# Strassen's scheme for 19 of 22 pairs of column blocks in the up projection of a hybrid decoder layer

## Chip, cores and metric

One core of one Trainium2 chip. The metric is the device time of one execution in microseconds.

## What is computed

One decoder layer on x of 1024 tokens by 1024 channels, float32: a mixer (gated DeltaNet, sparse attention and a convolution, with one input and one output projection), then the gated MLP, with which this case deals:

```python
def conv_gated_mlp(x, w_up, conv_w, w_down):      # x (1024, 1024), w_up (1024, 5632), conv_w (3, 5632), w_down (2816, 1024)
    h = causal_dwconv(x @ w_up, conv_w)           # 3 taps along the tokens, a channel at a time
    gt, val = jnp.split(h, 2, axis=-1)
    return (jax.nn.silu(gt) * val) @ w_down

h = rms_norm(x, norm_ffn_pre)
x = x + rms_norm(conv_gated_mlp(h, ffn_w_up, ffn_conv_w, ffn_w_down), norm_ffn_post)
```

## The kernel before, in words

The kernel is written by hand, with a queue for each engine and a semaphore wait before each instruction that needs one; `LATE` gives late stages semaphores that early ones have done with. In time order: input projection and convolutions, the mixer (a fixed interleaving of steps), output projection with both norms, up projection (from about 700 us), down projection (from about 1024 us).

**Operands in two parts.** A float32 matmul is made of two: each operand is split in a rounded high part and a low part. For a weight block, ACT writes the high part (`up_split_hi`, L1759: a copy with scale 1 - 1/64) and POOL the low part (`up_split_lo`, L1763: block minus high part). For the normed tokens h2, ACT writes h2_p (scale 1/64, L1657) and DVE h2_q (L1686). The matmul of high parts and that of low parts add up in PSUM to 1/64 of the product; the convolution's taps carry the factor 64.

**Up projection.** Channels lie on partitions, tokens along the free dimension. There are 22 pairs j of column blocks of 128: unit u = 2j is the gate block, u = 2j + 1 the value block. `up_products` (L1697) does a unit: 8 blocks k of the contraction, high and low, 2 halves of 512 tokens, so 32 matmuls of 128 x 512. A pair has four PSUM banks, and pairs take turns with the two sets of four. The first halves of units 0 to 2 are done in the stage before, between the last turns of tokens (`up_begin`); `up_pe` does the rest. After a unit ACT applies the last tap from PSUM into an SBUF tile (L1783), then splits the unit u + 3 (L1759), and after a value unit does the silu (L1795); DVE adds the other two taps, reading PSUM and the SBUF tile (L1814, L1817); POOL makes the low part of unit u + 3 (L1763) and after a value unit the product of gate and value (L1807), which stays in SBUF in `act_f[j]` for the down projection. SP loads unit u as soon as the staging tile is free (L1747), 512 KB. PE waits for the low part of its unit, and for the taps of the unit four back, whose banks it takes.

**Down projection.** Two halves of 512 tokens, m = 0 and 1, each with 22 blocks k: `kk` = 22 m + k. A step kk has 16 matmuls (L1980): four tiles of 128 tokens, high and low, two halves of 512 columns. ACT splits the high parts of the row block of w_down (L1849, 1024 columns) and of the activation (L1869, 512 columns), DVE the low parts (L1854 and L1873; POOL does L1854 for kk = 0 to 2). SP loads the rows of w_down (L1878) four steps ahead, and at kk = 8 and 37 the residual x1 (four tiles of 512 KB).

```python
            for k in ks:
                for w, x in ((up_p[up_slot(u)], h2_p), (up_q[up_slot(u)], h2_q)):
                    for h in halves:
                        ins = pe.matmul(up_ps[j % 2][:, g, h * 512:(h + 1) * 512], w[:, k], x[:, k, h * 512:(h + 1) * 512],
```

## Time and profile before

| | us |
|---|---|
| median of three runs | 1199.31 (1198.91 to 1199.84) |
| the profiled execution, its own time | 1199.23 |
| its span in the profile | 1197.2 |
| PE busy | 1148.0 (96%) |
| DVE busy | 707.1 (59%) |
| ACT busy | 566.3 (47%) |
| POOL busy | 367.0 (31%) |
| mean granted TensorE clock | 0.992 of full |

The time of an execution is 2.0 us longer than the span, which runs from the first to the last recorded instruction. Busy time is the time in which at least one instruction of an engine is under way; matmuls overlap one another, so a matmul's own duration (0.39 us for 512 columns) is longer than the distance from one to the next. A duration of an instruction runs from its issue to the engine to its end, with any wait inside the engine in it; waits on semaphores are not in it.

### The profile page before, as it was taken

To read this page: it belongs to the slowest core of one execution; us is meant where nothing else is said; L and a number is where in the kernel's file an instruction comes from. 1 tells how busy PE (TensorE), PEld (TensorE's weight loads), DVE (VectorE), ACT (ScalarE), POOL (GpSimd) and SP (SyncE) were. 2 spreads that over 40 slices of the span, in tenths; PEclk is the share of its full clock that TensorE was granted. 3 is DMA by queue.
4 is the path that set the end of the run, shared out by engine and by line. 5 is a ranking of instruction groups with operands and counts; after the bars stand their busy time and mean duration, and the time that the engine had idled before them with its cause. 6 is when DMAs were issued, how large, how long until landed. Compare 5 with 4: busy or idle time off the path is not lost.

```text
span 1197.2 us, 22879 instructions
## 1 busy us (share of the span) xinstructions
PE 1148.0 (96%) x9530; PEld 950.1 (79%) x9530; DVE 707.1 (59%) x982; ACT 566.3 (47%) x1053; POOL 367.0 (31%) x378
## 2 busy tenths in 40 slices
PE   5999999899999999999998999999999999999996
PEld 5878879788877877878767878888888888888885
DVE  5798976546668785767546744333333333655744
ACT  7544333447565556465565644333333334545443
POOL 2476346122122131120232025444555554200000
PEclk9999999999999999999998999999999999999999
DMA  8345121410000000000114452222222221654651
GB/s 252 84 113 182 59 52 27 103 31 22 3 22 22 2 22 22 2 2 2 38 52 160 146 171 82 77 71 71 71 71 71 73 80 58 235 169 123 228 193 71
DMA packets 104079, 99.86 MB, mean 83 GB/s; under 512 B 15413, under 2 KB 89385, under 8 KB 103977
## 3 DMA queue, kind: packets, MB, share of 16 engines
q1 hardware_dynamic: 102536, 93.15, 25.6%
q10 hardware_dynamic: 1440, 5.24, 1.1%
q8 instruction: 77, 1.26, 0.4%
q14 instruction: 26, 0.21, 0.1%
HBM read 85.24 MB, written 13.11 MB: 82 GB/s over the span
## 4 chain that ended last, share of the span: by engine, by line
PE 84%; DVE 10%; ACT 3%; DMA 1%; issue 1%; POOL 0%; ACTq 0%; DVEq 0%
PE psum L1697 26%; PE psum L1980 14%; PE psum L1344 8%; PE psum L2516 6%; PE psum L1591 5%; PE psum L1524 4%; PE psum L2556 4%; PE psum L1540 4%; DVE arena L2403 3%; PE psum L1505 2%; PE psum L1337 1%; PE psum L1271 1%; PE psum L1289 1%; PE psum L1504 1%; PE psum L1425 1%
## 5 line engine op out<-in xcount | busy, mean ns | idle before, releaser
L1697 PE MATMUL psum<-h_p,up_p 128*128 128x512 f32 x704 | 221.0, 390 | 1.3 <-DVE arena L1673 0.7
L1697 PE MATMUL psum<-h_q,up_q 128*128 128x512 f32 x704 | 220.7, 389 | 0.0
L1814 DVE SCALAR_TENSOR_TENSOR arena<-psum,arena 128x1023 f32<-128x1023 f32 x44 | 56.4, 1283 | 196.1 <-ACT arena L1783 196.1
L1763 POOL TENSOR_TENSOR up_q<-arena,up_p 128x1024 fp32r<-128x1024 f32 x44 | 105.9, 2407 | 212.8 <-ACT up_p L1759 212.8
L1697 PEld LDWEIGHTS psum<-h_p,up_p 128*128 128x128 f32 x704 | 132.2, 188 | 29.4 <-POOL up_q L1763 1.1
L1697 PEld LDWEIGHTS psum<-h_q,up_q 128*128 128x128 f32 x704 | 132.2, 188 | 27.3
L1783 ACT ACTIVATE arena<-psum,arena 128x1024 f32<-128x1024 f32 x44 | 49.1, 1117 | 198.9 <-PE psum L1697 198.9
L1344 PE MATMUL psum<-arena 64*64 64x64 f32 x3072 | 110.8, 221 | 2.6 <-DVE arena L1120 1.5
L1980 PE MATMUL psum<-dn_p,ap_p 128*128 128x512 f32 x352 | 110.2, 394 | 3.2 <-DVE ap_q L1873 3.2
L1344 PEld LDWEIGHTS psum<-arena 64*64 64x64 f32 x3072 | 97.5, 134 | 17.8 <-issue 6.8
L1980 PE MATMUL psum<-dn_q,ap_q 128*128 128x512 f32 x352 | 109.9, 394 | 0.0
L2516 PE MATMUL psum<-h_p,cm_p 128*128 128x512 f32 (+1 forms) x288 | 87.3, 374 | 4.1 <-ACT arena L2280 2.3
L1026 ACT ACTIVATE arena<-psum 128x384 f32<-128x384 f32 x132 | 60.4, 489 | 59.9 <-PE psum L1524 59.2
L2516 PE MATMUL psum<-h_q,cm_q 128*128 128x512 f32 (+1 forms) x288 | 86.7, 372 | 0.0
L1228 DVE TENSOR_REDUCE arena<-psum 128x1 f32<-128x640 f32 (+7 forms) x96 | 66.9, 705 | 32.0 <-PE psum L1509 30.2
L1854 DVE TENSOR_TENSOR dn_q<-arena,dn_p 128x1024 fp32r<-128x1024 f32 x41 | 51.4, 1254 | 57.0 <-ACT dn_p L1849 57.0
L1019 ACT ACTIVATE arena<-psum,arena 128x640 f32<-128x640 f32 (+7 forms) x96 | 67.1, 701 | 34.7 <-DVE arena L1228 34.0
L1980 PEld LDWEIGHTS psum<-dn_p,ap_p 128*128 128x128 f32 x352 | 66.6, 189 | 18.1 <-DVE dn_q L1854 3.6
L1849 ACT ACTIVATE dn_p<-arena 128x1024 fp32r<-128x1024 f32 x44 | 46.6, 1058 | 71.5 <-PE psum L1980 66.5
L1980 PEld LDWEIGHTS psum<-dn_q,ap_q 128*128 128x128 f32 x352 | 66.7, 189 | 14.8
L2403 DVE SCALAR_TENSOR_TENSOR arena<-psum,arena 128x1023 f32<-128x1023 f32 (+29 forms) x60 | 75.9, 1264 | 1.4
L2516 PEld LDWEIGHTS psum<-h_p,cm_p 128*128 128x128 f32 x288 | 54.9, 191 | 14.8 <-issue 2.5
(299 smaller groups left out, 2172.4 us busy)
## 6 DMA issues: line engine op xcount, KB each, us to landing
arena<-in_ffn_w_up SPq DMA_DIRECT2D x44, 512.0 KB, 3.8
arena<-in_ffn_w_down SPq DMA_DIRECT2D x44, 512.0 KB, 3.7
arena<-in_w_in SPq DMA_DIRECT2D x20, 512.0 KB, 3.8
arena<-in_x SPq DMA_DIRECT2D x16, 512.0 KB, 5.6
qkv_mid<-arena ACTq DMA_DIRECT2D x9, 512.0 KB
arena<-qkv_mid SPq DMA_DIRECT2D x8, 576.0 KB, 4.2
arena<-in_w_out SPq DMA_DIRECT2D x8, 512.0 KB, 3.8
x_mid<-arena SPq DMA_DIRECT2D x8, 512.0 KB, 3.3
```

Of the source, the lines that this page charges most:

```text
L1019: act.activation(probs(u), s_psum(u, n), ACT.Exp, bias=nmx[:, u % 2:u % 2 + 1], accum_out=psums[:, NH * kind + h:NH * kind + h + 1]).then_ ...
L1026: act.activation(pt[x % 2].rearrange("p g c -> p (g c)"), psum[:, bank, 0:GDIM], ACT.Copy).then_inc(done, 1)
L1228: v.tensor_reduce(nmx[:, u % 2:u % 2 + 1], s_psum(u, n), AX.X, ALU.max, negate=True).then_inc(sem("n_mx"), 1)
L1344: ins = pe.matmul(out[rows, h * CH:(h + 1) * CH], lhs[rows, h], rhs[rows, h], start=start, stop=True, skip_group_check=True)
L1591: ins = pe.matmul(wm_ps[WM_SLOT[t]][:, n * 512:(n + 1) * 512], x[:, k], w[:, n * 512:(n + 1) * 512], start=first and k == ks[0] and w is w ...
L1697: ins = pe.matmul(up_ps[j % 2][:, g, h * 512:(h + 1) * 512], w[:, k], x[:, k, h * 512:(h + 1) * 512], start=k == 0 and x is h2_p, stop=Tru ...
L1763: pool.tensor_tensor(up_q[up_slot(u)], up_st[up_slot(u)], up_p[up_slot(u)], ALU.subtract).then_inc(late("up_lo")[0], 1)
L1814: v.scalar_tensor_tensor(out=y[:, 1:S], in0=ps[:, 0:S - 1], scalar=tap(1, u), in1=y[:, 1:S], op0=ALU.mult, op1=ALU.add).then_inc(late("up_ ...
L1854: eng.tensor_tensor(dn_q[kk % 4], dn_st[kk % 4], dn_p[kk % 4], ALU.subtract).then_inc(late("dn_lo")[0] if kk < 3 else sem("dn_lv"), 1)
L1980: ins = pe.matmul(dn_ps[t % HT][:, n * 512:(n + 1) * 512], x[:, tok], w[:, n * 512:(n + 1) * 512], start=first and x is ap_p[s], stop=True ...
L2403: own.up(v.scalar_tensor_tensor(out=cacc[:, c, s:S], in0=glu[c][:, 0:S - s], scalar=w, in1=cacc[:, c, s:S], op0=ALU.mult, op1=ALU.add))
L2516: ins = pe.matmul(cm_ps[i % 2][:, c0:c1], w[:, k], x[:, k, c0:c1], start=k == 0 and x is h_p, stop=True, skip_group_check=True)
```

## The change

Pairs 0 to 2 stay as they are (`CLASSIC = 3`). For the pairs j = 3 to 21 the product [gate | value] = W^T h is taken as one of 2 x 2 blocks: gate and value block, lower and upper half of the contraction (kh), first and second half of the tokens (th). Seven products of half size (4 blocks k, high and low, 512 tokens: 8 matmuls) take the place of eight, in the variant with running sums: U = P1 + P6, U + P7 and U + P7 + P4 are formed in one PSUM bank, each copied out by ACT before the next product adds to it; P2 and P5 + P3 have banks of their own, which DVE adds.

- Once, during the classic pairs: h2 is laid out by halves of tokens; DVE rebuilds four quarters of it (`whole`, 128 x 2048 each) and forms differences (two on DVE, two on POOL), and the four combined operands T5, T6, T7 and T4 are split by ACT (`t_hi`) and DVE (`t_lo`).
- For each pair: SP loads both blocks (`pair_load`, 2 x 512 KB). DVE makes four sums of weight quarters (`weight_sum`, 128 x 512, all operands in SBUF). ACT and POOL split seven slabs of 128 x 512 (`split_mult_hi`, `split_mult_lo`), in a ring of five. ACT copies four results of 128 x 512 out of PSUM (`copied`), DVE adds three more from PSUM onto these (`added`). The convolution then reads the copy in SBUF (`c_a`, `c_b`) and no longer PSUM: ACT the last tap (`tap_a`, `tap_b`), DVE the other two, for gate and value. ACT does the silu, POOL the product.
- The product goes into one of two tiles, and SP stores it in DRAM (`spill`, 512 KB), but for pairs 0 to 2 and 21. In the down projection SP loads it back by halves of tokens (`act_reload`, 256 KB, 36 times), one with each step's load of w_down. The first three reloads wait until the last product of the up projection is done.

```diff
+CLASSIC = 3
+MULTS = [(1, CLASSIC)]
+for _j in range(CLASSIC, NF):
+    MULTS += [(i, _j) for i in (5, 6, 2, 7)] + [(1, _j + 1)] * (_j + 1 < NF) + [(i, _j) for i in (4, 3)]
+PRODUCTS = len(MULTS)
+RING = 5
...
+        mult_ps = lambda i, j: psum[:, 4 * (j % 2) + {1: 0, 6: 0, 7: 0, 4: 0, 2: 1, 5: 2, 3: 2}[i], :]
...
+        def split_mult_hi(act, i, j):
+            n = mult_at(i, j)
+            if n >= RING:
+                act.wait_ge(*late("up_mm", 2 * CLASSIC + n - RING + 1))
...
+            act.activation(slab_p[n % RING], sum_source(i, j), ACT.Copy, scale=1.0 - SPLIT_W).then_inc(late("up_hi")[0], 1)
...
+        def split_mult_lo(pool, i, j):
+            n = mult_at(i, j)
+            pool.wait_ge(*late("up_hi", 2 * CLASSIC + n + 1))
+            pool.tensor_tensor(slab_q[n % RING], sum_source(i, j), slab_p[n % RING], ALU.subtract).then_inc(late("up_lo")[0], 1)
...
+            t_hi(5, 0, "t_f", 3)
+            classic_tap(0)
+            up_split_hi(act, 3)
+            classic_tap(1)
+            up_split_hi(act, 4)
+            silu(0)
+            t_hi(7, 1, "t_pool", 1)
...
+            for j in range(CLASSIC, NF):
+                more = j + 1 < NF
+                if j > CLASSIC:
+                    tap_b(j - 1)
+                if more:
+                    split_mult_hi(act, 1, j + 1)
+                if j > CLASSIC:
+                    tap_a(j - 1)
+                else:
+                    silu(CLASSIC - 1)
+                split_mult_hi(act, 4, j)
+                copied(6, j)
+                split_mult_hi(act, 3, j)
+                if more:
+                    split_mult_hi(act, 5, j + 1)
...
+                copied(7, j)
+                if j > CLASSIC:
+                    silu(j - 1)
+                if more:
+                    split_mult_hi(act, 6, j + 1)
+                    copied(1, j + 1)
+                    split_mult_hi(act, 2, j + 1)
+                copied(4, j)
+                if more:
+                    split_mult_hi(act, 7, j + 1)
...
+            for j in range(CLASSIC, NF):
+                more = j + 1 < NF
+                if more:
+                    split_mult_lo(pool, 1, j + 1)
+                if j == CLASSIC:
+                    prod(CLASSIC - 1)
+                split_mult_lo(pool, 4, j)
+                split_mult_lo(pool, 3, j)
+                if more:
+                    split_mult_lo(pool, 5, j + 1)
...
+                if j > CLASSIC:
+                    prod(j - 1)
+                if more:
+                    for i in (6, 2, 7):
+                        split_mult_lo(pool, i, j + 1)
...
+            def conv(c, y, u, count):
+                v.wait_ge(*late("up_tap", count))
+                v.scalar_tensor_tensor(out=y[:, 1:S], in0=c[:, 0:S - 1], scalar=tap(1, u), in1=y[:, 1:S],
+                                       op0=ALU.mult, op1=ALU.add).then_inc(late("up_c1")[0], 1)
+                v.wait_ge(*late("up_c1", count))
+                v.scalar_tensor_tensor(out=y[:, 2:S], in0=c[:, 0:S - 2], scalar=tap(0, u), in1=y[:, 2:S],
+                                       op0=ALU.mult, op1=ALU.add).then_inc(late("up_conv")[0], 1)
+
+            def conv_b(j):
+                conv(c_b[j % 2], y_b[j % 2], 2 * j + 1, 2 * j + CONV_B)
...
+            def added(i, j):
+
+                mult_done(v, i, j)
+                src, dst = {2: (1, c_a[j % 2][:, left]), 5: (7, c_b[j % 2][:, right]), 3: (6, c_a[j % 2][:, right])}[i]
+                copy_done(v, src, j)
+                v.tensor_tensor(dst, dst, mult_ps(i, j), ALU.add).then_inc(late("c_add")[0], 1)
...
+            for j in range(CLASSIC, NF):
+                more = j + 1 < NF
+                if j > CLASSIC:
+                    added(3, j - 1)
+                if more:
+                    weight_sum(5, j + 1)
+                if j > CLASSIC:
+                    conv_b(j - 1)
+                    conv_a(j - 1)
+                added(2, j)
+                if more:
+                    weight_sum(6, j + 1)
...
+                added(5, j)
+                if more:
+                    weight_sum(7, j + 1)
+                    weight_sum(3, j + 1)
...
+            for n, (i, j) in enumerate(MULTS):
+                pe.wait_ge(*late("up_lo", 2 * CLASSIC + n + 1))
...
+                elif i in (6, 7):
+                    copy_done(pe, {6: 1, 7: 6}[i], j)
+                elif i == 4:
+                    copy_done(pe, 7, j)
+                    pe.wait_ge(*late("t_lo", 4))
+                elif i == 3:
+                    add_done(pe, 5, j)
+                for k in range(HT):
+                    for w, x in ((slab_p[n % RING], x_p[i]), (slab_q[n % RING], x_q[i])):
+                        ins = pe.matmul(mult_ps(i, j), w[:, k], x[:, k], start=k == 0 and x is x_p[i] and i not in (6, 7, 3, 4),
+                                        stop=True, skip_group_check=True)
+                ins.then_inc(late("up_mm")[0], 1)
...
+            for kk in range(4, DN):
+                dn_ready(sp, kk - 4)
                 down_load(sp, kk)
+                if kk + 2 in RELOADS:
+                    act_reload(sp, kk + 2)
```

## Rows read from the trace of the kernel before

**Rows 1.** The page's first part: busy us (share of the span) and instructions of each engine.
```profile
PE 1148.0 (96%) x9530; PEld 950.1 (79%) x9530; DVE 707.1 (59%) x982; ACT 566.3 (47%) x1053; POOL 367.0 (31%) x378
```

**Rows 2.** The chain of waits in order of time: start, us, engine, what, line.
```profile
714.10 1.23 DVE h_q L1686
715.38 308.60 PE psum L1697 x1360
1023.98 146.47 PE psum L1980 x640
1170.53 1.06 ACT dn_p L1849
1173.59 16.56 PE psum L1980 x64
```

**Rows 3.** Stretches of the up projection: busy us (instructions), clock, DMA share, GB/s.
```profile
core 0: us, PE busy (x) PEld busy (x) DVE busy (x) ACT busy (x) POOL busy (x), PEclk, DMA share, GB/s
...
900.00:950.00 50.00, 50.00 (x222) 41.40 (x222) 17.95 (x14) 17.30 (x17) 24.30 (x11) 1.00 0.24 70
```

**Rows 4.** Instructions in order of time, 866 to 869 us, DVE and POOL.
```profile
866.59 2.40 POOL L1763 TENSOR_TENSOR up_q<-arena,up_p 128x1024 fp32r<-128x1024 f32 x1 [4.84 <-ACT up_p L1759]
866.91 1.28 DVE L1817 SCALAR_TENSOR_TENSOR arena<-psum,arena 128x1022 f32<-128x1022 f32 x1
```

**Rows 5.** Instructions in order of time, 1026 to 1033 us, DVE and POOL.
```profile
1026.16 2.41 POOL L1854 TENSOR_TENSOR dn_q<-arena,dn_p 128x1024 fp32r<-128x1024 f32 x1 [4.85 <-ACT dn_p L1849]
...
1027.69 1.43 DVE L1873 SCALAR_TENSOR_TENSOR ap_q<-ap_p,arena 128x512 fp32r<-128x512 f32 x1
1028.51 2.88 POOL L1807 TENSOR_TENSOR arena<-arena 128x1024 f32<-128x1024 f32 x1
...
1029.96 2.51 DVE L1854 TENSOR_TENSOR dn_q<-arena,dn_p 128x1024 fp32r<-128x1024 f32 x1 [0.84 <-ACT dn_p L1849]
```

**Rows 6.** Durations by line: some with min/median/max ns, others busy us and mean ns.
```profile
L1697 PEld LDWEIGHTS psum<-h_p,up_p x704: 186/188/190, 699.6 to 1022.9; 128*128 128x128 f32 x176
...
L1854 DVE TENSOR_TENSOR dn_q<-arena,dn_p x41: 1210/1225/2511, 1030.0 to 1171.6; 128x1024 fp32r<-128x1024 f32 x41
...
L1873 DVE SCALAR_TENSOR_TENSOR ap_q<-ap_p,arena x44: 677/684/1431, 1020.4 to 1172.8; 128x512 fp32r<-128x512 f32 x44
...
L1160 DVE TENSOR_TENSOR arena<-arena x8: 546/548/1927, 327.4 to 631.4; 128x384 f32<-128x384 f32 x8
...
L1681 DVE SCALAR_TENSOR_TENSOR arena<-arena x8: 1275/1278/1285, 655.3 to 709.7; 128x1024 f32<-128x1024 f32 x8
...
L1807 POOL TENSOR_TENSOR arena<-arena x22: 2392/2412/2882, 727.5 to 1028.5; 128x1024 f32<-128x1024 f32 x22
...
L2076 POOL TENSOR_TENSOR vc_q<-arena,vc_p x2: 1287/1290/1293, 211.8 to 213.1; 128x512 fp32r<-128x512 f32 x2
...
L1133 DVE TENSOR_TENSOR arena<-psum,arena 128x384 f32<-128x384 f32 x40 | 22.2, 556 | 6.9 <-PE psum L1344 3.6
...
L1783 ACT ACTIVATE arena<-psum,arena 128x1024 f32<-128x1024 f32 x44 | 49.1, 1117 | 198.9 <-PE psum L1697 198.9
...
L1869 ACT ACTIVATE ap_p<-arena 128x512 fp32r<-128x512 f32 x44 | 27.0, 616 | 0.0
...
L1795 ACT ACTIVATE arena<-arena 128x1024 f32<-128x1024 f32 x22 | 23.1, 1052 | 0.0
...
L2122 ACT ACTIVATE kT<-psum 128x512 fp32r<-128x512 f32 x8 | 4.7, 592 | 0.2 <-PE psum L2142 0.2
```

**Rows 7.** Instructions in order of time, 630 to 634 us, POOL and DVE.
```profile
630.55 2.35 POOL L898 TENSOR_TENSOR wo_q<-arena,wo_p 128x1024 fp32r<-128x1024 f32 x1 [0.54 <-ACT wo_p L1051]
...
631.38 1.93 DVE L1160 TENSOR_TENSOR arena<-arena 128x384 f32<-128x384 f32 x1 [0.60 <-ACT arena L992]
```

**Rows 8.** A stretch of the down projection, columns as in rows 3.
```profile
1040.00:1060.00 20.00, 20.00 (x89) 16.39 (x88) 10.68 (x12) 8.12 (x11) 0.00 (x0) 1.00 0.74 276
```

**Rows 9.** The page's part on DMA issues: count, KB each, median us to landing.
```profile
x_mid<-arena SPq DMA_DIRECT2D x8, 512.0 KB, 3.3
```

**Rows 10.** PE after idling (instructions in order of time), and a stretch, columns as in rows 3.
```profile
1173.59 0.70 PE L1980 MATMUL psum<-dn_p,ap_p 128*128 128x512 f32 x2 [3.16 <-DVE ap_q L1873]
1174.13 0.99 PE L1980 MATMUL psum<-dn_q,ap_q 128*128 128x512 f32 x2
1174.92 1.05 PE L1980 MATMUL psum<-dn_p,ap_p 128*128 128x512 f32 x2
1175.78 1.05 PE L1980 MATMUL psum<-dn_q,ap_q 128*128 128x512 f32 x2
...
632.00:636.00 4.00, 2.64 (x8) 2.25 (x9) 3.18 (x4) 1.81 (x2) 0.89 (x1) 0.50 0.44 132
```

More of the change, by code:

```diff
@@ L284 @@
     "f_rs": ("tap0", 17),
-    "dn_hi": ("w_hi", 80),
+    "dn_hi": ("w_hi", 36 + 2 * CLASSIC + PRODUCTS),
     "ap_hi": ("rope_tab", 2),
@@ L317, with build @@
     "x1r3": ("gp_in", 32),
+    "sw_st0": ("x_in2", 64),
+    "sw_st1": ("x_in3", 64),
+    "t_f": ("k_lo", 8),
+    "t_pool": ("q_lo", 8),
+    "t_hi": ("k_hi", 8),
+    "t_lo": ("q_hi", 8),
+    "s_add": ("g_ss", 8),
+    "c_cp": ("g_rs", 8),
+    "c_add": ("c_ss", 8),
+    "act_st0": ("wck_in", 32),
+    "act_st1": ("wcv_in", 32),
 }
-def build(nc, a, out, scratch, qkv_mid):
+def build(nc, a, out, scratch, qkv_mid, act_mid):
     ctx = ExitStack()
@@ L1777, in up_act, with classic_tap @@
                 act.wait_ge(sem(f"x1_st{s}"), 16 * NT // 2)
-            for u in range(NU):
+            def classic_tap(u):
                 j, g = divmod(u, 2)
@@ new lines, in copied @@
+            def copied(i, j):
+                mult_done(act, i, j)
+                dst = {1: c_a[j % 2][:, left], 6: c_a[j % 2][:, right], 7: c_b[j % 2][:, right], 4: c_b[j % 2][:, left]}[i]
+                if i == 1 and j >= CLASSIC + 2:
+                    conv_done(act, j - 2, CONV_A)
+                if i == 1 and j == CLASSIC:
+                    act.wait_ge(*late("up_prod", 2))
+                if i == 7 and j >= CLASSIC + 2:
+                    conv_done(act, j - 2, CONV_B)
+                if i == 7 and j == CLASSIC:
+                    act.wait_ge(*late("up_prod", 3))
+                act.activation(dst, mult_ps(i, j), ACT.Copy).then_inc(late("c_cp")[0], 1)
@@ new lines, in tap_b, with tap_a @@
+            def tap_b(j):
+                add_done(act, 5, j)
+                copy_done(act, 4, j)
+                if j >= CLASSIC + 2:
+                    spilled(act, j - 2)
+                act.activation(y_b[j % 2], c_b[j % 2], ACT.Copy, scale=tap(2, 2 * j + 1)).then_inc(late("up_tap")[0], 1)
+            def tap_a(j):
+                add_done(act, 3, j)
+                add_done(act, 2, j)
+                if j >= CLASSIC + 2:
+                    act.wait_ge(*late("up_prod", j - 1))
+                act.activation(y_a[j % 2], c_a[j % 2], ACT.Copy, scale=tap(2, 2 * j)).then_inc(late("up_tap")[0], 1)
@@ new lines, in up_act @@
+            t_hi(5, 0, "t_f", 3)
[5 more added lines that the diff above has]
+            t_hi(7, 1, "t_pool", 1)
+            classic_tap(2)
+            up_split_hi(act, 5)
+            t_hi(6, 2, "t_f", 6)
+            classic_tap(3)
+            silu(1)
+            split_mult_hi(act, *MULTS[0])
+            classic_tap(4)
+            split_mult_hi(act, *MULTS[1])
+            split_mult_hi(act, *MULTS[2])
@@ L1823, in up_pe @@
         def up_pe(pe):
             pe.wait_ge(*late("v_lo", NT))
-            for u in range(NU):
+            for u in range(2 * CLASSIC):
                 pe.wait_ge(*late("up_lo", u + 1))
```

314 lines of the change are left out of this document (256 added, 58 removed).

## The prediction

> **What bounds the kernel now.** I read the page's busy shares first: PE is busy for 96% of the span [rows 1]. An average over stages proves little, so the chain of waits comes next. From 715.38 us it is one unbroken piece of up-projection matmuls of 308.60 us (1360 of them, 0.227 us each), followed directly by the down projection from 1023.98 us [rows 2]. So in the stage to be changed TensorE alone sets the pace, and an edit that removes matmuls shortens it, if no other engine then becomes slower than PE. The table of stretches says how much room the others have: in 50 us of the steady up projection DVE is busy 18.0, ACT 17.3 and POOL 24.3 us, with the clock at its full 2.4 GHz level [rows 3].
>
> One detail decides more than those shares. In the steady stage a POOL split (866.59 to 868.99) and a DVE tap (866.91 to 868.19) lie on top of each other and each takes its usual time, 2.40 and 1.28 us [rows 4]; that tap reads one operand from PSUM and one from SBUF. At the end of the stage, where DVE operates on two SBUF operands, it is otherwise. POOL works from 1026.16 to 1028.57; a DVE instruction issued at 1027.69 takes 1.43 us, not its median of 0.68, and ends 0.55 after POOL's end. The next POOL multiply, issued at 1028.51, takes 2.88 instead of 2.41 and ends 2.27 after DVE's end; the DVE subtraction behind it takes 2.51 instead of 1.23 and ends 1.08 after POOL's [rows 5, 6]. Far away, at 631.38, it is the same: 1.93 us instead of 0.55, ending 0.41 after POOL [rows 6, 7]. So a DVE instruction with two SBUF operands and a POOL tensor_tensor exclude each other; the one that waited runs 0.13 to 0.14 us shorter than alone once it is let in. Of the pairs of this sort that I read, none overlapped freely.
>
> **What the change does, part by part.**
> PE: a pair of column blocks has 2 x 8 x 2 x 2 = 64 matmuls of 512 columns; seven products of 4 x 2 make 56. At 0.227 us a pair goes from 14.5 to 12.7 us, and 19 x 8 = 152 matmuls fewer are 34.5 us less, the whole gain. Each product has weights of its own, where two matmuls in a row shared them, but a weight load stands beside every matmul already (as many as matmuls, 0.19 us each, under a pitch of 0.227 [rows 3, 6]): nothing.
>
> ACT per pair: seven slab splits of 512 columns at 0.62, four copies out of PSUM at 0.59, two taps at 1.12, one silu at 1.05 [rows 6]: 10.0 us, under 12.7.
>
> DVE per pair: three additions of a PSUM bank to one SBUF operand (0.56 for 384 columns, so some 0.69 for 512), four sums of weight blocks with both operands in SBUF (between 0.55 for 384 and 1.23 for 1024: 0.68), and the four convolution taps of 1.28 [rows 6]. 2.1 + 2.7 + 5.1 = 9.9 us, also under 12.7. But the taps now read c_a or c_b, which lie in SBUF, where they read PSUM. Eight DVE instructions a pair now have two SBUF operands, 7.8 us; there was none.
>
> POOL per pair: seven slab subtractions of 512 columns at 1.29 and one product of 2.41 [rows 6]: 11.5 us, under 12.7 by itself.
>
> The sum that matters is of the two that exclude each other: 11.5 + 7.8 = 19.3 us a pair, above both 12.7 and the old 14.5. From this go 0.135 us for each of the 16 instructions that had to wait; if they take turns throughout, 17.15. Do they? DVE's queue is in order: sum, addition, four taps, addition and so on, and with POOL always having a slab to do, each two-operand DVE instruction waits for one POOL instruction, eight against eight. DVE's three additions and the waits of the others fall beside POOL's work. Behind a held tap stand DVE's later additions, and PE's last product of a pair waits for one of them (P5), so PE idles some 5 us a pair. Bounds: 17.15 (turns throughout, nothing idle) and 20.3 (no gain at hand-over, 1 us in which neither works). I take 17.9, two of three hand-overs with the gain, being nearer to the rows, in which every waiting instruction had it.
> The Trainium skill, "SBUF — State Buffer", Who interferes with whom, says that a VectorE instruction with two SBUF inputs and a GpSimd instruction that reads SBUF hold a shared port as an exclusive lock, and the second to issue fully blocks until the first is done. The trace agrees that it is exclusive; read literally the rule would give 19.3 us a pair, since it knows no shortening, where the rows give 17.15 with turns throughout. The measured 0.13 us decides.
>
> Start of the stage: the classic units need 3 x 3.6 + 3 x 7.3 = 32.7 us of PE, as before. Beside them come, on DVE, four halves of 2048 columns rebuilt, two differences, four low parts (each 2048 columns, two SBUF operands, about 2.3 us: 0.68 + 3 x 0.53), four weight sums; on POOL two differences of 2048 (2.41 + 2 x 1.12 = 4.6 each), three splits and three products of 2.41 and five slabs. Exclusive work: 25.7 + 30.3 = 56 us, a bound from below; DVE's queue with all POOL work before it is 41 + 30 = 71, from above. Walking the queues in order with these durations, unit 3 waits for its low part until 729, unit 4 until 743, unit 5 until 751 (POOL's 4.6 us difference and DVE's sums alternate), the first slab is ready at 765, and the last product of the first pair ends 68 us after 715.4. ACT, too, holds unit 0's tap behind a high part that waits for three DVE instructions.
> Then 18 x 17.9 = 322: the up projection ends at 715.4 + 68 + 322 = 1105.6, against 1024.0: +81.6 us.
>
> End of the stage: DVE's last addition, four taps and their waits for POOL's two splits of w_down end 8.5 us after the last product, and the third operand of the down projection is split only then, where PE wants it after 7.3 us. I take +3, from 0 to 8.
> DMA: per pair 1 MB in and 0.5 MB out in 17.9 us is 88 GB/s, against 276 in the busiest stretch [rows 8]. The spill has a whole pair (about 17 us) until its buffer is wanted, and a store of 512 KB lands in 3.3 us [rows 9]: nothing. Down projection: 0.75 MB per 3.65 us step is 215 GB/s, near that 276 where 2.5 MB of residuals come too. Reloads are issued some four steps ahead; I take 0, up to +6. SP queues the reload behind the weights of the step and both have that cover.
>
> Sum: the profiled execution took 1199.23 us (0.1 below the median of the runs shown, so the same). 1199.2 + 81.6 + 3 = **1284 us**.
>
> **Rivals.**
> *Faster: no exclusion for these taps.* They take a per-partition scalar, unlike the blocked rows. If they ran beside POOL as the PSUM taps do, PE would bound: 1199.2 - 34.5, plus about 5 for start and end, **1170 us**. The place is the four taps and four sums of each pair, and the sign turns where 4.8 of the 19.3 us overlap. Against it: four blocked instructions of both operation kinds, none free. Chance 0.05.
> *Exclusion with idle time.* The queues wait for one another (silu for the taps, slabs for weight sums), the port lies idle 1 us or so, hand-overs gain little: 20 us a pair, 1199.2 + 68 + 18 x 20 - 308.6 + 3 = **1322 us**. For it: ACT's order ties slabs behind silu, silu behind the fourth tap. Chance 0.20.
> *The clock.* After 3.16 us of idling PE came back at 1173.59 with a pitch of 0.43 us, the 1.2 GHz level, for some 4 us; and the stretch 632 to 636 was granted half [rows 2, 10]. The new stage leaves PE idle about 5 us a pair, in two or three pieces. If these bring the clock down, a product takes 3.4 us instead of 1.8; all seven at that level would need 24 us. With half of them so: 21 us a pair, **1340 us**. Against it: the pieces are each under 3 us, and DVE is free only 2 us after the last product, which hides one slow product. Chance 0.12.
>
> **How the numbers follow.** The forecast has 0.60. Its own low end is 17.15 us a pair and a start of 56: 1199.2 + 56 + 309 - 308.6 = 1255. The range 1255 to 1335 holds it, the idle case and the milder part of the clock case; left out are the faster rival, 0.03 for something between, and the worst of the clock. About 0.2% (2.4 us) is what measurement tells from no change; the only case near zero is a part of that 0.03, so 0.05 faster, 0.02 same, 0.93 slower.
>
> **What the profile after would show.** 1256 up-projection matmuls, not 1408. The convolution taps at a mean near 2.4 us instead of 1.28, the slab subtractions well above 1.29 (2 or more), the additions from PSUM unchanged near 0.69; in any steady 50 us DVE and POOL both over 90% busy, PE near 70% with its idle time put down to POOL's slab parts and DVE's additions, ACT half idle. If taps stay at 1.28 beside POOL work, my argument falls and the time is near 1170. If the taps are as said but PE's granted clock is under 0.9, it is the third rival. If the difference comes after 1110 us, the reloads were mispriced.

## The result and the profile after

The changed kernel takes 1263.53 us (median of four runs, 1262.95 to 1265.03), the kernel before beside it 1199.11 us (four runs, 1198.88 to 1199.84). The ratio is 1.0537, 95% interval 1.052 to 1.0554: slower by 64.4 us. The forecast was 1284, with a range from 1255 to 1335.

The page's first part for the kernel after, as in [rows 1] (the span is 1263.3 us, the profiled execution's own time 1265.03):

```profile
PE 1152.8 (91%) x9359; PEld 941.7 (75%) x9378; DVE 958.5 (76%) x1125; ACT 655.8 (52%) x1228; POOL 565.7 (45%) x475
```

TensorE (PE) has 171 fewer recorded matmuls (152 fewer in the program) and yet no less busy time; DVE has 251 us more of it, POOL 199 us more. The steady stretch, in the same columns as [rows 3], with one of the down projection below:

```profile
core 0: us, PE busy (x) PEld busy (x) DVE busy (x) ACT busy (x) POOL busy (x), PEclk, DMA share, GB/s
850.00:900.00 50.00, 43.29 (x170) 34.49 (x169) 49.79 (x34) 28.18 (x42) 49.91 (x24) 0.91 0.31 95
...
1110.00:1130.00 20.00, 20.00 (x89) 16.49 (x88) 9.54 (x11) 8.49 (x11) 0.00 (x0) 1.00 0.98 367
```

POOL and DVE are both busy for over 99.5% of this stretch, with 24 and 34 instructions in 50 us. PE does 170 matmuls in that time where it did 222. Two engines that look full with so few instructions are the sign to look at durations. By line, with the smallest, median and largest ns of one instruction, against the durations of [rows 6]:

```profile
L1910 POOL TENSOR_TENSOR slab_q<-arena,slab_p x133: 1269/2251/2290, 763.8 to 1076.2; 128x512 fp32r<-128x512 f32 x133
...
L2117 DVE TENSOR_TENSOR arena<-arena x76: 682/1720/2880, 760.9 to 1068.8; 128x512 f32<-128x512 f32 x76
...
L2077 DVE SCALAR_TENSOR_TENSOR arena<-arena x38: 1273/2308/2322, 786.6 to 1091.7; 128x1023 f32<-128x1023 f32 x38
L2077 DVE SCALAR_TENSOR_TENSOR arena<-psum,arena x6: 1270/1271/1282, 726.5 to 770.1; 128x1023 f32<-128x1023 f32 x6
...
L2124 DVE TENSOR_TENSOR arena<-arena,psum x57: 671/674/689, 778.5 to 1086.1; 128x512 f32<-128x512 f32 x57
```

A tap (L2077) takes 1.27 us where it reads PSUM, and 2.31 us at the median where it reads the copy in SBUF; its smallest is still 1.27. The additions that read PSUM (L2124) stay between 0.671 and 0.689 us, whatever POOL does. A slab subtraction of 1.29 us takes 2.25. What lies in those durations shows in the instructions in order of time (start, us, engine, line; POOL's seven slab parts of a pair, one behind the other, are one row):

```profile
849.91 14.05 POOL L1910 TENSOR_TENSOR slab_q<-arena,slab_p 128x512 fp32r<-128x512 f32 x7
...
853.83 2.31 DVE L2077 SCALAR_TENSOR_TENSOR arena<-arena 128x1023 f32<-128x1023 f32 x1
856.17 2.20 DVE L2080 SCALAR_TENSOR_TENSOR arena<-arena 128x1022 f32<-128x1022 f32 x1
858.29 2.31 DVE L2077 SCALAR_TENSOR_TENSOR arena<-arena 128x1023 f32<-128x1023 f32 x1
860.64 2.19 DVE L2080 SCALAR_TENSOR_TENSOR arena<-arena 128x1022 f32<-128x1022 f32 x1
862.75 0.68 DVE L2124 TENSOR_TENSOR arena<-arena,psum 128x512 f32<-128x512 f32 x1
```

Four taps and the slabs beside them take turns: from 853.83 to 862.75 is 8.92 us for four taps and four slabs, 2.23 us for each couple, where the two would take 1.28 + 1.29 = 2.57 alone. So the two hand-overs of a couple (an engine that waited for the other is let in) give back 0.17 us each on the mean. Read one by one, a held tap ends 1.08 us after the slab before it (0.20 less than its time alone), a held slab 1.15 us after the DVE instruction before it (0.14 less), a held weight sum 0.55 us after a slab (0.13 less), the product 2.23 us after a sum (0.18 less). Four taps, four sums, seven slabs and one product make 4.32 + 2.20 + 8.05 + 2.23 = 16.80 us, the whole period of a pair: the two engines take turns with nothing left over. The Trainium skill, "SBUF — State Buffer", Who interferes with whom, calls it an exclusive lock in which the second instruction waits for the first to finish. The exclusion is here, but by this rule a couple would take 2.57 us.

The waits between 780 and 1080 us (engine and line, what it waits for; us in total, times, longest us) show who pays:

```profile
ACT arena L1940 <- DVE arena L2080: 54.0, 18, 4.5
...
PE psum L2204 <- DVE arena L2124: 41.5, 17, 3.6
```

PE waits once a pair, 2.4 us at the mean (41.5 / 17), for the addition P5 that stands in DVE's queue behind the held taps. The chain of waits, which was one piece of matmuls in [rows 2], now goes over the taps, pair after pair:

```profile
716.51 7.56 PE psum L1744 x32
...
853.90 2.24 DVE arena L2077
856.17 2.20 DVE arena L2080
858.37 2.24 DVE arena L2077
860.81 1.94 issue
...
865.04 3.84 DVE arena L2117 x2
...
870.69 2.25 DVE arena L2077
...
1083.05 3.02 PE psum L2204 x8
...
1099.75 135.71 PE psum L2382 x592
...
1238.60 17.64 PE psum L2382 x64
```

(The "issue" of 1.94 us is the fourth tap, which the chain does not name; the instructions above show it.) In the chain the first tap of one pair starts at 853.90 and that of the next at 870.69: 16.8 us a pair. The difference of the two spans, 1263.3 - 1197.2 = 66.1 us, is put together as follows.

| part | before | after | difference |
|---|---|---|---|
| all ahead of this piece of the up projection | 715.4 | 716.5 | +1.1 |
| from there to the end of pair 3's last product (before: to 18 pairs from the end) | 47.5 | 67.3 | +19.8 |
| the last 18 pairs | 18 x 14.51 = 261.1 | 18 x 16.79 = 302.2 | +41.1 |
| from the end of the last up matmul to the end of the span | 173.2 | 177.3 | +4.1 |

(Before, the last 18 pairs are the last 1152 matmuls of the up projection. After, pair 3's last product ends at 783.8 and the last of all at 1086.1 us.) Six tenths of the loss are the steady pairs (41.1 of 66.1), three tenths the start (19.8).

### The profile page after: what moved, and what is told of

The parts are those of the page before. It is cut to its first block, busy times and chain, and to the rows that moved or that the text cites. A ratio compares the mean times of both kernels' runs of the same rounds, so it can differ in the third digit from the quotient of the medians.

```text
span 1263.3 us, 23393 instructions
## 1 busy us (share of the span) xinstructions
PE 1152.8 (91%) x9359; PEld 941.7 (75%) x9378; DVE 958.5 (76%) x1125; ACT 655.8 (52%) x1228; POOL 565.7 (45%) x475
## 3 DMA queue, kind: packets, MB, share of 16 engines
q8 instruction: 76, 1.25, 0.4%
## 4 chain that ended last, share of the span: by engine, by line
PE 62%; DVE 26%; issue 6%; ACT 3%; POOL 2%; DMA 1%; DVEq 0%; ACTq 0%; POOLq 0%
PE psum L2382 12%; PE psum L2923 9%; PE psum L1391 8%; DVE arena L2077 6%; DVE arena L2117 5%; PE psum L1638 4%; PE psum L2204 4%; PE psum L1571 4%; PE psum L2963 3%; PE psum L1587 3%; DVE arena L2080 3%; PE psum L1552 2%; DVE arena L2124 2%; DVE arena L2810 2%; PE psum L1384 1%
## 5 line engine op out<-in xcount | busy, mean ns | idle before, releaser
L1910 POOL TENSOR_TENSOR slab_q<-arena,slab_p 128x512 fp32r<-128x512 f32 x133 | 262.6, 2008 | 1.0 <-ACT slab_p L1905 1.0
L2204 PE MATMUL psum<-h_p,slab_p 128*128 128x512 f32 x304 | 132.7, 437 | 52.0 <-DVE arena L2124 43.9
L2204 PE MATMUL psum<-h_q,slab_q 128*128 128x512 f32 x304 | 130.1, 428 | 0.0
L2117 DVE TENSOR_TENSOR arena<-arena 128x512 f32<-128x512 f32 x76 | 120.5, 1604 | 1.3 <-POOL slab_q L1910 1.3
L2204 PEld LDWEIGHTS psum<-h_p,slab_p 128*128 128x128 f32 x304 | 63.1, 207 | 75.1 <-issue 51.1
L1905 ACT ACTIVATE slab_p<-arena 128x512 fp32r<-128x512 f32 x133 | 83.2, 626 | 51.7 <-DVE arena L2117 31.6
L2204 PE MATMUL psum<-t_p,slab_p 128*128 128x512 f32 x228 | 93.2, 409 | 0.0
L2204 PE MATMUL psum<-t_q,slab_q 128*128 128x512 f32 x228 | 92.2, 405 | 0.0
L2077 DVE SCALAR_TENSOR_TENSOR arena<-arena 128x1023 f32<-128x1023 f32 x38 | 85.5, 2250 | 0.0
L2080 DVE SCALAR_TENSOR_TENSOR arena<-arena 128x1022 f32<-128x1022 f32 x38 | 83.7, 2201 | 1.4
L2382 PEld LDWEIGHTS psum<-dn_p,ap_p 128*128 128x128 f32 x352 | 67.3, 192 | 20.8 <-DVE dn_q L2237 4.8
```

Source lines behind the costliest of these rows:

```text
L1905: act.activation(slab_p[n % RING], sum_source(i, j), ACT.Copy, scale=1.0 - SPLIT_W).then_inc(late("up_hi")[0], 1)
L1910: pool.tensor_tensor(slab_q[n % RING], sum_source(i, j), slab_p[n % RING], ALU.subtract).then_inc(late("up_lo")[0], 1)
L2077: v.scalar_tensor_tensor(out=y[:, 1:S], in0=c[:, 0:S - 1], scalar=tap(1, u), in1=y[:, 1:S], op0=ALU.mult, op1=ALU.add).then_inc(late("up_c ...
L2080: v.scalar_tensor_tensor(out=y[:, 2:S], in0=c[:, 0:S - 2], scalar=tap(0, u), in1=y[:, 2:S], op0=ALU.mult, op1=ALU.add).then_inc(late("up_c ...
L2117: v.tensor_tensor(out, x, y, op).then_inc(late("s_add")[0], 1)
L2204: ins = pe.matmul(mult_ps(i, j), w[:, k], x[:, k], start=k == 0 and x is x_p[i] and i not in (6, 7, 3, 4), stop=True, skip_group_check=True)
```

## The experiments

Two theories stood against each other, as the expectations name them. The theory of the prediction: a DVE instruction with two SBUF operands and a POOL instruction that reads SBUF never work at the same time, and their summed durations are the pair's period. Its rivals: PE's idling and its lowered clock, a tap that is slow by itself when it reads SBUF, and the spill. But for e5 repeated and e9, which have five runs each, an experiment has one run, beside one run of the kernel before on the same chip: 1199.86 us for e1, e3, e4 and e5, and 1199.76 us for e2, e6, e7 and e8.

### e1: the taps read PSUM

```diff
             def conv_b(j):
+                if j < NF - 2:
+                    return conv_spare(4 * (j % 2) + 3, y_b[j % 2], 2 * j + 1, 2 * j + CONV_B)
                 conv(c_b[j % 2], y_b[j % 2], 2 * j + 1, 2 * j + CONV_B)
```

`conv_spare` does the same two instructions, 1022 columns each, but with the unused fourth PSUM bank of the pair as first operand (511 columns, read twice); `conv_a` likewise. The convolution of pairs 3 to 19 thus has another input; all copies and additions stay.

> The changed kernel, but for pairs 3 to 19 the two DVE taps read a spare PSUM bank (1022 columns) in place of the copies in SBUF; everything else, DVE's number of instructions and their widths too, is kept. The values of h are then not those of the reference. Theory (exclusion): only POOL's 11.5 us and the four weight sums' 2.7 us of a pair still exclude each other, 14.2 us less 0.17 for each of 8 hand-overs, so a pair takes 13.0 to 14.0 us in place of 16.8, the taps are back at 1.28 us beside POOL work, and the time is 1209 to 1225 us. Rival (DVE's queue or ACT's order sets the pace, and the long durations have another cause, the traffic of DMA or PE): taps stay above 2 us, the pair stays at 16 to 17 us, and the time at 1255 us or above.

Measured: 1199.0 us, 10 us under the expected range. The stretch, the taps (busy us, mean ns, idle before) and the chain:

```profile
850.00:900.00 50.00, 49.99 (x218) 40.20 (x216) 49.72 (x44) 35.37 (x54) 49.97 (x32) 1.00 0.38 116
```

```profile
L2088 DVE SCALAR_TENSOR_TENSOR arena<-psum,arena 128x1022 f32<-128x1022 f32 x68 | 85.4, 1276 | 1.2
```

```profile
910.82 12.94 PE psum L2218 x56
```

The taps are back at 1.28 us, PE is busy throughout, and a pair takes 12.94 us, less than the 13.0 to 14.0 expected. The kernel gets back 1265.03 - 1199.0 = 66.0 us, as much as it had lost, by where the taps' first operand lies; all of that is in the steady pairs, since the start is as long as before (67.1 us). The taps of the last two pairs still read SBUF.

What is left of the exclusion is four weight sums beside seven slabs and a product: 11.5 + 2.7 = 14.2 us less eight hand-overs of 0.17, 12.85 by that reckoning. It still sets the pace, by a little. POOL is busy for 49.97 of the 50 us, DVE's sums have a mean of 1.60 us, for the most part waiting, and once a pair PE waits for the addition of P5 before its last product. PE's own 56 matmuls would take 12.7 us. The wait is 0.25 us a pair; e5, whose pair is the same, shows it below.

### e4: the kernel before with taps that read SBUF

```diff
                 v.wait_ge(*late("up_tap", u + 1))
+                if j >= 2:
+                    v.wait_ge(*late("up_prod", 1))
+                    ps = act_f[0]
```

From pair 2 on DVE's two taps take their first operand from an SBUF tile that is written once, so the values of h are not those of the reference. Nothing else of the change is made here.

> The kernel before, but from pair 2 on the first of the two DVE taps of a unit and the second read an SBUF tile (the product of pair 0) in place of PSUM; the values of h are not those of the reference. Theory (exclusion): four taps of 1.28 and POOL's three instructions of 2.41 are 12.3 us that exclude each other, under the 14.5 us that PE needs for a pair, so single instructions get longer (taps 1.28 to a mean of 1.6 to 2.4 us, some POOL instructions over 2.41) and the time stays within 0.3% of 1199 us. Rival (a tap with both operands in SBUF is slower by itself, or only the Strassen stage's extra traffic makes them long): all taps alike, or none longer, beside POOL work and away from it.

Measured: 1200.6 us, one run, against 1199.86. PE stays at 50.00 of 50 us. The taps by line and one meeting with POOL:

```profile
L1817 DVE SCALAR_TENSOR_TENSOR arena<-arena x40: 1283/1284/1286, 742.3 to 1025.1; 128x1023 f32<-128x1023 f32 x40
...
L1820 DVE SCALAR_TENSOR_TENSOR arena<-arena x40: 3298/3301/3306, 743.6 to 1026.4; 128x1022 f32<-128x1022 f32 x40
```

```profile
866.55 2.55 POOL L1763 TENSOR_TENSOR up_q<-arena,up_p 128x1024 fp32r<-128x1024 f32 x1 [4.70 <-ACT up_p L1759]
866.88 3.30 DVE L1820 SCALAR_TENSOR_TENSOR arena<-arena 128x1022 f32<-128x1022 f32 x1
```

This shows the two engines most clearly. In [rows 4] a tap issued at 866.91 into POOL's work took 1.28 us; here one issued at 866.88 takes 3.30 and ends 1.08 us after POOL. The first tap of each unit, with two SBUF operands as well, is issued while POOL is idle and takes 1.28 us all forty times; where POOL is issued in its last 0.3 us, POOL is the one that is held (2.55 us in place of 2.41). So a tap from SBUF is not slow by itself. And 4 x 1.28 + 2 x 2.41 + 2.41 = 12.3 us of exclusive work a pair lie under the 14.5 of PE: +0.7 us, which one run does not tell from nothing (nine runs of the kernel before lie between 1199.18 and 1200.39). So the exclusive work cost nothing measurable at 12.3 us a pair beside 14.5 of PE, and in e1, just above PE's 12.7, it cost 0.25 us a pair; in the kernel after it is 16.8 beside 12.7.

### e3: PE kept busy

```diff
                 elif i == 3:
+                    if j < NF - 2:
+                        for k in range(HT):
+                            for r in range(2):
+                                pe.matmul(psum[:, 4 * (j % 2) + 3, :], x_p[1][:, k, 0:P], x_p[1][:, k], start=k == 0 and r == 0,
+                                          stop=True, skip_group_check=True)
                     add_done(pe, 5, j)
```

Eight more matmuls a pair into the unused bank, in the place where PE waits.

> The changed kernel with eight more matmuls of 512 columns in each of pairs 3 to 19, into a spare PSUM bank, put ahead of PE's wait before the last product (1.8 us of the 4 us or so that PE idles). Theory (exclusion of DVE and POOL): PE's idling is slack, a pair stays at 16.8 us, the time stays at 1262 to 1268 us and the granted clock in 800 to 1050 us rises from 0.91 to 1.00. Rival (the lowered clock costs time): with the full clock the slow products come back to 1.8 us and a pair gets shorter by 1 us or more, 1230 to 1250 us. Second rival (PE bounds through its waits): each pair gets 1.8 us longer, 1290 us or above.

Measured: 1265.93 us, the same as without them (the profiled execution after is 1265.03). In the kernel after, PE ran slow soon after its wait:

```profile
882.04 0.47 PE L2204 MATMUL psum<-h_p,slab_p 128*128 128x512 f32 x1 [2.21 <-DVE arena L2124]
...
882.59 0.63 PE L2204 MATMUL psum<-h_p,slab_p 128*128 128x512 f32 x1
883.02 0.63 PE L2204 MATMUL psum<-h_q,slab_q 128*128 128x512 f32 x1
```

From 882.59 to 883.02 is 0.43 us, the pitch of the 1.2 GHz level as in [rows 10], after 2.21 us without work. Of the first 16 such waits, 13 were followed by 5 to 12 matmuls at this pitch and three by none; the granted clock of the stretch was 0.91. With the gap filled the clock is full, and the pair is as long as it was:

```profile
850.00:900.00 50.00, 45.83 (x191) 34.86 (x190) 49.79 (x34) 27.25 (x42) 49.97 (x25) 1.00 0.31 95
```

```profile
871.11 2.25 DVE arena L2077
...
887.98 2.25 DVE arena L2077
```

The pair still takes 887.98 - 871.11 = 16.87 us. The lowered clock was there and cost nothing: PE had some 4 us a pair to spare. It also explains most of why PE looks 87% busy in the kernel after, where the prediction had near 70%: it has 12.7 us of work at full clock in 16.8, 76%, and most of the rest of its busy time is the same work done slowly.

### e2: half of POOL's slab work

```diff
-            pool.tensor_tensor(slab_q[n % RING], sum_source(i, j), slab_p[n % RING], ALU.subtract).then_inc(late("up_lo")[0], 1)
+            pool.tensor_tensor(slab_q[n % RING][:, 0:2], sum_source(i, j)[:, 0:2], slab_p[n % RING][:, 0:2], ALU.subtract).then_inc(late("up_lo")[0], 1)
```

POOL makes the low part of the first two blocks of a slab only; the matmuls of the other two take it in the place of their own.

> The changed kernel, but POOL makes the low part of half of each slab only (256 of 512 columns) and PE uses that half twice; the result of h differs. The taps read SBUF as in the changed kernel. Theory (exclusion; the time is the sum of what POOL and DVE do with the shared access): a slab takes POOL about 0.73 us in place of 1.29, so 5.1 + 2.4 + 7.8 = 15.3 us less 16 hand-overs of 0.17 make 12.7 us, beside PE's 12.7: 12.8 to 13.6 us a pair and 1190 to 1210 us, although each DVE tap still has two SBUF operands and is still held up, by less (mean 1.7 to 1.9 us in place of 2.25). Rival (two SBUF operands cost DVE a fixed penalty, whatever POOL does): taps stay at 2.2 us, DVE's queue takes as long as before, the pair stays at 15 us or more, 1230 us or above.

Measured: 1200.37 us. The taps start at 850.71 and 863.90, 13.19 us a pair. By line:

```profile
L2077 DVE SCALAR_TENSOR_TENSOR arena<-arena x38: 1273/1757/2805, 785.2 to 1027.8; 128x1023 f32<-128x1023 f32 x38
```

DVE's work is untouched, its taps still read SBUF, and their median falls from 2.31 to 1.76 us because POOL's pieces beside them are shorter. Halving seven instructions of 1.29 us takes some 3.9 us from the exclusive work and 3.6 from the period. Taking work from either of the two engines shortens the pair, as it must if they share one resource. PE is busy for 49.1 of 50 us here, so the pair is again a little above PE's 12.7.

### e8: POOL writes, but reads nothing

```diff
-            pool.tensor_tensor(slab_q[n % RING], sum_source(i, j), slab_p[n % RING], ALU.subtract).then_inc(late("up_lo")[0], 1)
+            q = slab_q[n % RING].bitcast(F32)
+            pool.memset(q, 0.0).then_inc(late("up_lo")[0], 1)
```

The low part of the weights is zero in the Strassen pairs.

> The changed kernel, but POOL fills each slab's low part with zeros (an instruction that writes SBUF and reads nothing) in place of the subtraction; the low part of the weights is left out of the products. An operation of 128 x 384 of this kind took 0.42 us in the kernel before, so about 0.55 us here. Theory A (the exclusion is of reads): the fills overlap with DVE freely, mean 0.55 us, and only taps and sums that meet POOL's product of 2.4 us are held up, so the tap's median is 1.28 us. Theory B (any SBUF access of POOL excludes): fills that meet a tap wait for it, mean 0.9 us or above, and taps that meet a fill come out at 1.6 to 1.8 us. In both PE bounds, 12.7 us a pair and 1183 to 1200 us; the durations tell them apart.

Measured: 1187.36 us. By line, and a meeting of the two engines in order of time:

```profile
L1911 POOL MEMSET slab_q<- x133: 517/527/537, 763.6 to 1002.2; 128x512 f32 x133
...
L2078 DVE SCALAR_TENSOR_TENSOR arena<-arena x38: 1276/1279/2822, 782.8 to 1016.6; 128x1023 f32<-128x1023 f32 x38
```

```profile
848.79 1.28 DVE L2078 SCALAR_TENSOR_TENSOR arena<-arena 128x1023 f32<-128x1023 f32 x1
849.86 0.53 POOL L1911 MEMSET slab_q<- 128x512 f32 x1 [1.77 <-ACT slab_p L1905]
850.10 1.28 DVE L2081 SCALAR_TENSOR_TENSOR arena<-arena 128x1022 f32<-128x1022 f32 x1
```

The fill at 849.86 lies on top of the end of one tap and the start of the next, and all three take their time alone; of 133 fills none is longer than 0.537 us. POOL's product, which reads two SBUF operands, is still excluded in the same run: a weight sum issued 0.28 us after it takes 2.89 us in place of 0.68. So DVE's two SBUF operands exclude POOL's reads and not its writes. The Trainium skill, "SBUF — State Buffer", Who interferes with whom, speaks of a GpSimd instruction that reads SBUF and excepts one that only writes it; this holds here, for `scalar_tensor_tensor` too. In the chain 56 matmuls take 12.69 us, PE's own period:

```profile
849.79 110.39 PE psum L2205 x487
```

### e5: the results stay in PSUM, with nothing left out

e1 says what would help; it can be had with the right values. A pair uses three of its four banks. If the additions write to PSUM in place of SBUF and the banks are laid out so that c_b and c_a are two adjacent banks each, the taps read PSUM, and the fourth copy of ACT drops out:

```diff
-        mult_ps = lambda i, j: psum[:, 4 * (j % 2) + {1: 0, 6: 0, 7: 0, 4: 0, 2: 1, 5: 2, 3: 2}[i], :]
+        mult_ps = lambda i, j: psum[:, 4 * (j % 2) + {1: 0, 6: 0, 7: 0, 4: 0, 2: 2, 5: 3, 3: 3}[i], :]
+        cb_ps = lambda j: psum[:, 4 * (j % 2):4 * (j % 2) + 2, :].rearrange("p a b -> p (a b)")
+        ca_ps = lambda j: psum[:, 4 * (j % 2) + 2:4 * (j % 2) + 4, :].rearrange("p a b -> p (a b)")
...
-                v.tensor_tensor(dst, dst, mult_ps(i, j), ALU.add).then_inc(late("c_add")[0], 1)
+                out = psum[:, 4 * (j % 2) + {2: 2, 5: 1, 3: 3}[i], :]
+                v.tensor_tensor(out, dst, mult_ps(i, j), ALU.add).then_inc(late("c_add")[0], 1)
...
-                conv(c_b[j % 2], y_b[j % 2], 2 * j + 1, 2 * j + CONV_B)
+                conv(cb_ps(j), y_b[j % 2], 2 * j + 1, 2 * j + CONV_B)
...
-                    copy_done(pe, 4, j - 2)
+                    conv_done(pe, j - 2, CONV_B)
```

PE now waits for the taps of the pair two back before it takes the banks again, and so does the down projection.

> The changed kernel with the results of a pair put together in PSUM: each of DVE's three additions writes to a PSUM bank (the pair has four), the fourth copy of ACT falls away, and ACT's and DVE's taps read PSUM as in the kernel before. Theory (exclusion): as in e1, 14.2 us less hand-overs exclude each other in a pair, against PE's 12.7: 13.0 to 14.0 us a pair, up projection ends near 1020 to 1040 us, time 1195 to 1220 us. Rival (another cause): 1255 us or above. If DVE's own queue binds through its waits for POOL, the pair comes out nearer to 14.5, the time near 1225 us.

Measured: 1191.36 us, 3.6 us under the expected range. Five runs were expected as follows:

> The kernel of e5 (results put together in PSUM) again, timed against the kernel before. Theory: a pair takes 12.9 us, which is the 14.2 us that still exclude each other less 8 hand-overs of 0.17, beside PE's 12.7, so the time is 1190 to 1193 us, 0.5 to 0.8% faster than the kernel before.

Measured: median 1191.55 us (1190.19 to 1193.03) against 1199.86 us of nine runs of the kernel before; ratio 0.9932, interval 0.992 to 0.9945. This version is faster than both kernels, by 8.3 and by about 72 us. Its stretch, its lines and its chain:

```profile
850.00:900.00 50.00, 49.97 (x218) 40.16 (x217) 49.72 (x43) 33.17 (x51) 49.99 (x32) 1.00 0.40 121
```

```profile
L2078 DVE SCALAR_TENSOR_TENSOR arena<-psum,arena x44: 1268/1272/1283, 725.9 to 1018.3; 128x1023 f32<-128x1023 f32 x44
```

```profile
715.90 7.56 PE psum L1746 x32
...
845.24 12.94 PE psum L2206 x56
...
1013.09 2.07 PE psum L2206 x8
```

The up projection from 715.90 to 1015.2 takes 299.3 us, where the kernel before took 308.6. The last 18 pairs are 232.1 of it against 261.1, 29.0 us gained; the start is 67.2 against 47.5, 19.7 us given back. Only 9.3 of the 29.0 us remain. That e5 is 8 us faster than e1 with the same 12.94 us a pair lies for the most part in e1's last two pairs, whose taps read SBUF: its last product ends 6.3 us later.

PE's row of 49.97 us hides a short wait, since a matmul's duration is longer than its pitch. In order of time:

```profile
896.25 0.68 DVE L2126 TENSOR_TENSOR psum<-arena,psum 128x512 f32<-128x512 f32 x1
...
896.68 0.39 PE L2206 MATMUL psum<-h_q,slab_q 128*128 128x512 f32 x1
...
897.08 0.47 PE L2206 MATMUL psum<-h_p,slab_p 128*128 128x512 f32 x1
897.39 0.39 PE L2206 MATMUL psum<-h_q,slab_q 128*128 128x512 f32 x1
```

The addition of P5 ends at 896.93 and the last product of the pair starts 0.15 us behind it, 0.40 us after the matmul before in place of 0.23; the next matmul follows after 0.31. These two steps, once a pair, are the 0.25 us between 12.94 and e8's 12.69. A weight sum and a slab in turns take 1.70 us in e5 (0.55 + 1.15), and slabs that follow each other start 1.26 us apart. Four sums, three held slabs, the held product and four free slabs are 2.20 + 3.45 + 2.23 + 5.04 = 12.92 us. So DVE and POOL together still set e5's pair, with PE just under them.

### e6, e9: the start

In e5 the start is the larger part of what could still be won. e6 gives POOL's two 2048-column differences, which take it 6.57 and 4.62 us in the kernel after, to DVE:

```diff
-            pool.wait_ge(*late("t_f", 4))
-            pool.tensor_tensor(t_f[7], t_f[6], t_f[7], ALU.subtract).then_inc(late("t_pool")[0], 1)
...
+            v.wait_ge(*late("t_f", 4))
+            v.tensor_tensor(t_f[7], t_f[6], t_f[7], ALU.subtract).then_inc(late("t_pool")[0], 1)
```

> The kernel of e5 (results in PSUM) with one change at the start of the stage: the two differences of 2048 columns are made by DVE in 2.3 us each and no longer by POOL in 4.6 us each. Theory (the start, too, is set by what excludes each other): 4.7 us less of it, and POOL is free for the splits of units 4 and 5; the first slab is ready 3 to 7 us earlier and the time is 1184 to 1189 us. Rival (DVE's queue sets the start, since it now has 4.6 us more): no gain or a loss, 1190 to 1196 us.

Measured: 1193.01 us, one run, which is inside e5's spread of 1190.19 to 1193.03. No gain is seen: POOL starts the first slab at 763.72 us, with DVE making the differences, against 763.22 in e5. e9 is e5 with ACT's split of the first slab ahead of the second silu, and POOL's low part of it ahead of the second product:

```diff
-            silu(1)
             split_mult_hi(act, *MULTS[0])
+            silu(1)
...
+            split_mult_lo(pool, *MULTS[0])
             prod(1)
-            for n in range(RING):
+            for n in range(1, RING):
```

> The kernel of e5 with two orders changed at the start: ACT splits the first slab ahead of the silu of pair 1, and POOL makes that slab's low part ahead of the product of pair 1, for which it stood idle for 4.8 us (754.97 to 759.77 in e5). Theory (the start is set by a few instructions in POOL's and DVE's queues): PE can run the first product while DVE makes the first sums, so the stage is 1 to 3 us shorter than in e5, 1188 to 1191 us. Rival (DVE's weight sums set the second product, whatever comes before): same as e5 within 0.7 us.

Measured: 1190.3 us (1189.94 to 1191.8, five runs), 1.25 us under e5 at the median with overlapping spreads: inconclusive. The first product starts earlier, at 760.63 us against 764.99 in e5, and the next then waits for its slab:

```profile
765.06 0.60 PE L2207 MATMUL psum<-t_p,slab_p 128*128 128x512 f32 x1 [2.34 <-POOL slab_q L1912]
```

### e7: the spill

e5 with 16 columns stored and reloaded for each tile in place of all; the down projection reads the products of pairs 0 to 2 for the others.

```diff
-            sp.dma_start(act_mid[j], y_b[j % 2]).then_inc(late(f"act_st{j % 2}")[0], 16)
+            sp.dma_start(act_mid[j][:, 0:16], y_b[j % 2][:, 0:16]).then_inc(late(f"act_st{j % 2}")[0], 16)
```

> The kernel of e5 with spill and reload cut to 16 columns each (SP issues as many DMAs as before); the down projection reads the products of pairs 0 to 2 in place of the reloaded ones, so its result differs. Theory (the spill and its reload are hidden): within 1.5 us of e5, 1189.5 to 1192.5 us, though DMA moves 18 MB less and its share in 1020 to 1050 us falls from 1.0 to 0.7 or so. Rival (the reloads hold up the start of the down projection): 1183 to 1189 us, PE idle between 1010 and 1030 us gone.

Measured: 1191.55 us, with e5 at 1191.36. A stretch of the down projection, e7's:

```profile
1020.00:1050.00 30.00, 29.53 (x130) 23.91 (x129) 17.60 (x20) 16.40 (x21) 2.40 (x1) 1.00 0.82 279
```

and the same of e5:

```profile
1020.00:1050.00 30.00, 29.55 (x130) 24.02 (x129) 17.53 (x20) 16.96 (x21) 2.40 (x1) 1.00 1.01 385
```

DMA carries 385 GB/s in e5 and 279 in e7, with PE at the same 130 matmuls. So the spill and the reloads cost nothing that one run shows (0.2 us), though the DMA engines are full in this stretch.

## Why the prediction was right, and where its size was off

**What bounds: right.** PE set the pace before, and after the change it is POOL and DVE together. Of the loss, e1 takes back all by moving one operand of the taps; by taking away from POOL's side e2 takes back nearly as much (64.7 us) and e8 more (77.7).

**PE's part: right.** The gain of the missing eighth product is real: in e8 a pair takes 12.69 us and in e1 and e5 12.94, where 12.7 was reckoned and 14.5 stood before. It went to waste because PE was no longer the bound.

**The three engines by themselves: right.** Additions from PSUM 0.674 us (0.69 reckoned), weight sums 0.68 and slabs 1.27 at their smallest, a tap 1.27. DVE and POOL each have less than 12.7 us of work a pair; nothing in a list of busy shares of the kernel before would have warned.

**The exclusion: right, its period mis-sized.** The step that failed is the term of the pair: "I take 17.9, two of three hand-overs with the gain". Measured is 16.8 us. Two things were off. The queues took turns throughout, with nothing idle, and every hand-over gave something back, where a third of them was written off: that is 0.7 of the 1.1 us. And a hand-over gives back 0.16 us on the mean of the 16 (19.3 - 16.8 = 2.5), 0.20 for a held tap, and not the 0.135 read from the few meetings of [rows 5 to 7], where no tap was among them: that is the other 0.35. So the bound from below should have been 16.8 and not 17.15. 18 x (17.9 - 16.79) is 20.0 us, the whole distance from the forecast of 1284 to the 1265 of the profiled execution; the other terms together are 1 to 2 us the other way. The own low end of 1255 lies under the measured 1263.5 only because it also had a start of 56 us, where 67 were measured. With the start of the forecast, 68 us, it would have been 1268, above the result. That the low end held is luck: two errors of opposite sign.

**The start: right.** 68 us were reckoned, 67.3 measured. POOL's second difference took the 4.6 us of the sum, the first 6.57, in turns with DVE. In e5 and e1, where the taps of the later pairs read PSUM, the start is as long, 67.2 and 67.1 us. What bounds it is not fully settled: the chain there runs over DVE's rebuilt halves and low parts, and in e6 shifting work between the two queues did not measurably shorten it.

**The end: right.** +3 reckoned, +4.1 measured from the last matmul; the down projection's third operand comes late, at 1099.75, as said.

**DMA: right at 0.** e7. The page's issues show that 18 stores land in 2.6 us each and 36 reloads in 5.5; one step of the down projection is 3.65 us, and they are issued at least four steps ahead.

**The rivals.** "No exclusion for these taps" is refuted by e4 and by the 2.31 us of L2077. Its price of 1170 us was too low besides: it had about 5 us for start and end, and e8, with PE as the bound, takes 1187. "Exclusion with idle time" at 20 us a pair did not come: the turns themselves make up the 16.8 us. "The clock": its premise held, 0.43 us pitch after an idle piece of 2.2 us and 0.91 in the stretch, and its consequence did not, as e3 shows. It missed that PE's slow matmuls run in time that PE has to spare. The forecast's own test for it, a clock under 0.9, does not tell the cases apart: 0.90 to 0.91 was measured with no effect on the time.

## What to carry to other kernels

Before an operand of a DVE instruction is moved from PSUM to SBUF, add up DVE's instructions with two SBUF operands and POOL's that read SBUF, as if they were one engine, less some 0.16 us for each hand-over; if the sum is above the period of the bounding engine, that sum is the new period, however idle both look. The cure is in the operands and not in the order: leave one in PSUM, as e5 does, and add up again, since in e5 what is left of the exclusion still sets the pace by 0.25 us a pair. A change that saves work in a steady loop must also pay for its start; here 20 us of 29 were spent on it.

## What the runs showed of the hardware that was not expected

- An instruction that waited for the other engine's access then runs 0.13 to 0.20 us shorter than alone, at every hand-over of a long alternation: 0.20 for a tap, 0.13 for a weight sum, 0.14 for a slab, 0.18 for the product. An estimate from [rows 6] fits: DVE's 0.548 us for 384 columns and 1.225 for 1024 are 1.06 ns a column and a fixed 0.14; POOL's 1.290 for 512 and 2.412 for 1024 are 2.19 ns and a fixed 0.17. If only the part by columns is exclusive, a held tap would end 1.08 us after POOL (measured 1.08), a sum 0.54 (0.55), a slab 1.12 (1.15) and the product 2.24 (2.23). That is only argued; no run here separates the two parts.
- POOL's writes alone do not take part: 133 fills of 128x512 between 0.517 and 0.537 us, beside taps with two SBUF operands.
- An idle piece of some 2.2 us a pair was followed in most pairs by 5 to 12 matmuls at a pitch of 0.43 us in place of 0.23, and with eight matmuls in that piece the clock was 1.00; neither changed the time of a kernel that PE does not bound (1265.93 against 1265.03 us).
- Not tried: another number of classic pairs, the weight sums on another engine, and a start without the rebuilt halves.
